# Denser gate scatter, and sparse rows of 2048 spread over peer_u and peer_v

## The reference

```python
idx = jnp.take_along_axis(cand_idx, pos, axis=-1)      # [256, 8, 16] experts
g = jax.nn.softmax(top_s, axis=-1)
u = expert_u[ic]
a = jnp.einsum('cd,ced->ce', xc, u)
w = gc * jax.nn.gelu(a)
y = jnp.einsum('ce,ced->cd', w, expert_v[ic])
```

## Time and profile before

| | us |
|---|---|
| median of 3 runs | 3195.71 (3194.75 to 3195.85) |
| profiled execution | 3201.04, its span 3199.2 |

### The profile page before, as it was taken

One profiled execution on the slowest core, in us unless ns is written; L12 is line 12 of the kernel. 1 busy time (PEld: TensorE's weight loads), 2 busy tenths in 40 slices (PEclk: granted clock), 3 DMA queues, 4 the chain that ended last, 5 costly groups with the idle time before them and its releaser, 6 DMA issues.

```text
span 3199.2 us, 44410 instructions
## 1 busy us (share of the span) xinstructions
PE 3096.1 (97%) x17208; PEld 2746.4 (86%) x17208; DVE 2202.6 (69%) x3156; ACT 1511.8 (47%) x2039; POOL 664.6 (21%) x499
## 2 busy tenths in 40 slices
PE   9889999999988779999999999999999999999998
PEld 7778899999888779999999988888888888888886
DVE  6776589997777368888876665655465655555556
ACT  5655455544344344444444544455444544444443
POOL 0010007776888732222210000000000000000000
PEclk9999999999999989999999999999999999999999
DMA  7465568889999689999877655555665666666664
GB/s 261 139 237 205 185 212 230 225 225 288 319 316 317 163 295 332 331 331 331 303 252 216 206 187 174 160 181 173 192 202 167 205 189 191 193 192 188 192 191 150
DMA packets 228019, 723.35 MB, mean 226 GB/s; under 512 B 55696, under 2 KB 64928, under 8 KB 218688
## 3 DMA queue, kind: packets, MB, share of 16 engines
q1 hardware_dynamic: 170784, 598.72, 57.7%
q0 software_dynamic: 56880, 121.75, 13.1%
q10 hardware_dynamic: 144, 0.05, 0.0%
HBM read 687.75 MB, written 31.57 MB: 225 GB/s over the span
## 4 chain that ended last, share of the span: by engine, by line
PE 76%; POOL 9%; DVE 8%; issue 4%; ACT 1%; DMA 1%; DVEq 0%; ACTq 0%; SPq 0%; POOLq 0%
PE PS L1928 75%; POOL scr_g L3150 8%; DVE wlo L2464 3%; PE PS L2023 1%; POOL M L3177 1%; ACT whi L2192 1%; DMA M<-scr_g 1%; DVE M L2787 0%; DMA scr_g<-M 0%; DVE TMP L2885 0%; DVE TMP L2879 0%; DVE M L2791 0%; DVE Y L2789 0%; DVE M L2785 0%; DVE M L2793 0%
## 5 line engine op out<-in xcount | busy, mean ns | idle before, releaser
L2464 DVE TENSOR_TENSOR wlo<-raw,whi 128x1024 fp32r<-128x1024 f32 x1101 | 1341.8, 1222 | 607.4 <-ACT whi L2192 604.9
L2192 ACT ACTIVATE whi<-raw 128x1024 fp32r<-128x1024 f32 x1101 | 1154.4, 1057 | 947.7 <-PE PS L1928 915.2
L1928 PE MATMUL PS<-BB,whi 128*128 128x448 f32 (+1 forms) x4352 | 1025.0, 378 | 30.8 <-ACT whi L2192 28.3
L1928 PEld LDWEIGHTS PS<-BB,whi 128*128 128x128 f32 x4352 | 787.2, 191 | 113.9 <-issue 31.3
L1928 PE MATMUL PS<-whi,AA 128*128 128x512 f32 x3072 | 780.5, 395 | 5.2 <-DVE AA L2518 1.8
L1928 PEld LDWEIGHTS PS<-whi,AA 128*128 128x128 f32 x3072 | 571.6, 188 | 122.9 <-DVE AA L2470 2.7
L1928 PEld LDWEIGHTS PS<-BB,wlo 128*128 128x128 f32 x4352 | 579.6, 192 | 56.9 <-DVE wlo L2464 32.9
L1928 PE MATMUL PS<-BB,wlo 128*128 128x224 f32 (+1 forms) x4352 | 585.4, 278 | 28.7 <-DVE wlo L2464 28.6
L3150 POOL DMA_INDIRECT scr_g<-M x256 | 452.7, 1768 | 92.2 <-issue 76.8
L1928 PE MATMUL PS<-wlo,AA 128*128 128x512 f32 x1536 | 417.4, 390 | 0.0
L1928 PEld LDWEIGHTS PS<-wlo,AA 128*128 128x128 f32 x1536 | 288.8, 188 | 61.0
(11 more groups left out here) (275 smaller groups left out, 1856.4 us busy)
## 6 DMA issues: line engine op xcount, KB each, us to landing
raw<-in_peer_u SPq DMA_DIRECT2D x256, 512.0 KB, 4.7
raw<-in_peer_v SPq DMA_DIRECT2D x256, 512.0 KB, 5.2
raw<-in_w_in SPq DMA_DIRECT2D x160, 512.0 KB, 3.7
raw<-in_w_up SPq DMA_DIRECT2D x128, 512.0 KB, 4.3
raw<-in_w_down SPq DMA_DIRECT2D x128, 512.0 KB, 4.3
raw<-in_w_out SPq DMA_DIRECT2D x64, 512.0 KB, 4.2
raw<-in_w_in_a SPq DMA_DIRECT2D x32, 512.0 KB, 4.4
raw<-in_peer_w_q SPq DMA_DIRECT2D x32, 512.0 KB, 4.4
```

What stands on the lines that cost most here:

```text
L1928: return e.matmul(outp, l, r, start=start, stop=stop)
L2192: e.activation(whi[:, n % NH, :], raw[:, n % NR, :], ACT.Copy).then_inc(s_hi, 1)
L2464: e.tensor_tensor(wlo[:, n % NH, :], raw[:, n % NR, :], bf(whi[:, n % NH, :]), ALU.subtract).then_inc(s_lo, 1)
```

## The change

- The gates and addresses of both go to one array `RG[t]`. For t = 1 a new step `pack_rows` on ACT's DMA queue, two steps after the routing of those heads, lays the 96 dense tokens' columns out over 128 partitions (`packs`), with 12 DMAs, and with 4 more does what `route_rows` did on POOL. A round of t = 1 is then 12 scatters of 128 rows instead of 16 of 96, so 224 in all. They wait for the packing to land.
- Dots and adds take 2048 columns in one instruction. `sparse_sum` disappears.
- `EARLY` = 22 of the 32 rows are dotted over peer_u, now at one step and then two steps for each row, the dot two rows behind its gather. The other 10 and gelu and gate move into `sparse_rest` over peer_v, ahead of the adds, with two buffers and 2 + 2 steps a row. The fetches wait for the first 22 dots instead of all 32.
- In peer_v the guard that waited for the adds stands before chunk 7, block 5, and `v_end` waits for them in its task.

```diff
+SETS = ((96, 32),)
+NSP = sum(n for _, n in SETS)
-    SCATTERS, DOT_PACE, ADD_PACE = 1.5, ((1, 1), (1, 1)), (2, 2)
+    SCATTERS, EARLY, PACE = 1.5, 22, ((1, 2), (2, 2))
...
-                    for k in range(16):
+                    n_k = 16 if t == 0 else TL // 8
+                    for k in range(n_k):
...
                         if t == 1:
-                            go("route_rows", g, fresh("POOL", routed[-1][2]))
-                            for _ in range(GSP):
+                            for _ in range(2):
+                                yield
+                            go("pack_rows", g, fresh("ACT", ready))
+                            for _ in range(sum(128 // n for _, n in groups) + sum(128 // n for _, n in SETS)):
                                 mark = landing(f"routes_landed{g}")
                             sp_routed[g] = mark
+                            ready = [mark]
+                        routed.append((t, 4 * g, ready))
...
+            def row_stream(table, cols, bufs, pace, start, use):
+                landed, lead = {}, len(bufs) - 1
+                free = {b: [start, last_row[0]] for b in bufs}
+                for n in range(len(cols) + lead):
+                    if n < len(cols):
+                        b = bufs[n % len(bufs)]
+                        go("gather", table, cols[n], b, fresh("POOL", sp_routed[0], sp_routed[1], t_z, free[b]))
+                        landed[n] = landing(f"rows_landed{b % 3}")
+                    for _ in range(pace[0]):
+                        yield
+                    if n >= lead:
+                        b = bufs[(n - lead) % len(bufs)]
+                        last_row[0] = use(cols[n - lead], b, landed[n - lead])
+                        free[b] = [last_row[0]]
+                    for _ in range(pace[1 + n % (len(pace) - 1)]):
+                        yield
...
+                yield from sparse_dots(0, EARLY, (0, 1, 2), PACE[0], bar)
+                early.append(last_row[0])
...
-                go("fetch", n, fresh("POOL", w, a_written[n], g_written, sp_weighed))
+                go("fetch", n, fresh("POOL", w, a_written[n], g_written, early))
...
+            def sparse_rest():
+                start = [bar, g_written, early]
+                yield from sparse_dots(EARLY, NSP, (2, 3), PACE[1], start)
+                go("sparse_gelu", fresh("ACT", last_row))
...
+                    yield from row_stream(1, cols, (2, 3), PACE[1], start, add)
...
-                if c == 7:
-                    while not sp_added:
+                for db in range(8):
+                    while (c, db) == (7, 5) and not sp_added:
                         step()
...
+            def pack_rows(g, ready):
+                for mark in ready:
+                    e.wait_ge(*mark)
+                rows = RG[1][:, 128 * g:128 * g + 128]
+                per = TL // 8
+                cols = packs[:, 8 * per * g:8 * per * g + 8 * per].rearrange("p (h c) -> p h c", h=8)
+                for q, n in groups:
+                    parts = rows.rearrange("p (h s r) -> p h s r", h=8, s=128 // n)
+                    for i in range(128 // n):
+                        e.dma_start(cols[n * i:n * i + n, :, q // 8:q // 8 + n // 8], parts[q:q + n, :, i, :]
+                                    ).then_inc(sem(f"routes_landed{g}"), 16)
...
+            def sparse_dot(m, b, ready):
+                for mark in ready:
+                    e.wait_ge(*mark)
+                x = row_bufs[b]
+                e.tensor_tensor_reduce(out=x, in0=x, in1=z_all, scale=1.0, scalar=0.0, op0=ALU.mult, op1=ALU.add,
+                                       accum_out=sp_dot[:, m:m + 1]).then_inc(sem("sparse_step"), 1)
```

More of the change, by code:

```diff
@@ L1239, in walk, with z_side @@
             bar, t_z, sp_weighed = [], [], []
-            def z_side():
+            last_row, z_of = [None], [None]
+            def z_side(i, b, start):
+                go("load_gain2", b, fresh("POOL", start, last_row))
+                a = landing("z_landed")
+                for _ in range(4):
+                    yield
+                go("z_rows", b, r2, fresh("DVE", t_r2, t_R, a, bar))
+                a = up("DVE", "sparse_step")
+                yield
+                go("z_spread", i, b, fresh("POOL", a, start, last_row))
+                for _ in range(128 // SETS[i][1]):
+                    mark = landing("z_landed")
+                t_z[:] = [a, mark]
+                z_of[0] = i
@@ new lines, in sparse_dots, with dot @@
+            def sparse_dots(first, end, bufs, pace, start):
+                def dot(m, b, landed):
+                    go("sparse_dot", m, b, fresh("DVE", landed, t_z))
+                    return up("DVE", "sparse_step")
+                for i in range(len(SETS)):
+                    cols = [m for m in range(first, end) if columns[m][0] == i]
+                    if cols and z_of[0] != i:
+                        yield from z_side(i, bufs[0], start)
+                    if cols:
+                        yield from row_stream(0, cols, bufs, pace, start, dot)
@@ L1242, in z_side, with first_dots @@
+            early = []
+            def first_dots():
                 while not bar:
                     yield
[L1244 to L1281, removed]
@@ L1397, in walk @@
                 if u == 59:
-                    while not sp_weighed or len(g_written) < 2:
+                    while not early or len(g_written) < 2:
                         step()
@@ L1408, in walk @@
             nA, sp_added = [], []
[L1410 to L1423, removed]
-                yield
[L1425 to L1429, removed]
-                    yield
[L1431 to L1434, removed]
@@ L1437, in walk, with v_end @@
+            tasks.append(sparse_rest())
             ssv = stat(16).rearrange("p (t c) -> p t c", t=2)
             r3, ss_v, t_r3, rows_in_place = stat(2), stat(2), [], []
-            def v_end(db, ready):
+            def v_end(db, summed):
                 k0 = 2 * db
+                while not sp_added:
+                    yield
+                ready = [summed, sp_added]
                 bank, bfree = yield from wait_for(misc)
@@ L2334, in gelu @@
                 act(gels[gi].rearrange("p (m n) -> p m n", m=2), usum[ti], ACT.Gelu_apprx_tanh, "gelu")
+            def pack_rows(g, ready):
[9 more added lines that the diff above has]
+                                    ).then_inc(sem(f"routes_landed{g}"), 16)
+                for j, (p0, n) in enumerate(SETS):
+                    both = rows[p0:p0 + n, :].rearrange("p (a s m) -> p a s m", a=2, s=128 // n)
+                    a = columns.index((j, 0)) + n // 2 * g
+                    for i in range(128 // n):
+                        e.dma_start(routes[n * i:n * i + n, :, a:a + n // 2], both[:, :, i, :]
+                                    ).then_inc(sem(f"routes_landed{g}"), 16)
             def sparse_gelu(ready):
@@ L3161, in z_spread @@
+            def z_spread(i, b, ready):
                 for mark in ready:
                     e.wait_ge(*mark)
-                for s in range(GSP):
-                    e.dma_start(z_all[NSP * s:NSP * s + NSP, :], u_rows[1][P0:128, :]).then_inc(sem("z_landed"), 16)
-            def route_rows(g, ready):
+                p0, n = SETS[i]
+                for k in range(128 // n):
+                    e.dma_start(z_all[n * k:n * k + n, :], row_bufs[b][p0:p0 + n, :]).then_inc(sem("z_landed"), 16)
@@ L3167, in route_rows, with gather @@
+            def gather(table, m, b, ready):
                 for mark in ready:
                     e.wait_ge(*mark)
[L3169 to L3179 removed]
```

142 lines of the change are left out of this document (71 added, 71 removed).

## The result

The changed kernel takes 3174.25 us (median of 5, 3165.67 to 3176.62), beside 3194.75 for the kernel before (median of 5). The ratio is 0.9925, with a 95% interval of 0.9914 to 0.9936: 20 to 28 us less. The forecast was 37 less.

The account below looks back on a forecast made before the run. POOL's queue of scatters and gathers was taken to bound peer_u. Its 74.7 us loss goes to 29 + 8, plus 1, minus 2: 37 less, 3159 us from 3195.71; likeliest 3145 to 3172, range 3133 to 3182.

Parts of the forecast that it names:

- Bound and mechanism: In peer_u, POOL's scatters and gathers set the pace (44.5 us lost) and end late at the tail (29.5 us lost).
- Scatters: On POOL, t = 1 goes from 128 scatters of 96 rows to 96 of 128: 224 in all, about 56 us less.
- Wait of a scatter: A POOL scatter waits for the rest of a running DVE dot or split: mean 0.43 us before, 0.50 after.
- A unit with dots: In peer_u, POOL needs 11.9 us a unit (bounds 10.5 and 12.1); 29 us lost replaces 44.5.
- Tail: At peer_u's end, last scatter about 1042 plus packing cost, before the gate is wanted; the 29.5 us gap goes.
- the better clock: In the first unit of peer_v, the chain of fetches keeps its steps; 1 us was given for TensorE's better clock.
- Packing: 16 DMA issues on ACT, twice, about 7 us each with 4.5 covered: 4 a time, 8 us, bounds 0 and 20.
- rival B: Packing costs much more (20 us) or POOL is still late at the fetch: 3182, middle 3176; chance 0.18.
- the sum: Over the whole kernel, 74.7 us goes to 29 + 8; plus 1, minus 2: 37 less, 3159.
- peer_v: 10 more gathers and dots, then 32 wide adds, done by u57; 0 to 8 us, taken as 2.
- rival C: Wide DVE instructions delay splits and stop TensorE, 78 us against 37 gained: slower, some 3235; chance 0.05.
- The observables: Expected signs: no gate wait, unit ends 11.9 apart, scatter mean near 2.0, some over 3 us, ACT blocks, peer_v 10.1 a unit.

Follow-up runs that it names:

- r5: The changed kernel with 1.6 scatters a step until the first gathers are planned and 1.25 after, for 1.5 throughout: 3156.71 us, ratio 0.9866.
- r2: The kernel before with only the dense packing and the 224 scatters, its dots untouched: 3198.73 us, ratio 0.9996.
- r3: The changed kernel with the old 256 scatters and rows laid out by POOL, nothing packed on ACT: 3195.12 us, ratio 0.9986.
- r8: The changed kernel with each dot of 2048 as two instructions of 1024, back to back: 3167.33 us, ratio 0.9895.
- r9: The changed kernel with every dot over the first 32 of 2048 columns only, gathers and waits kept: 3143.36 us, ratio 0.9827.
- r6: The changed kernel with the scatter rates of r5 and the packing issued four DMAs at a time: 3157.83 us, ratio 0.9847.
- r7: As r6, with the first expert gates planned after unit 60 of peer_u instead of 61: 3168.55 us, ratio 0.9906.
- r4: The changed kernel with the 16 packing DMAs issued four at a time in a task of their own: 3170.60 us, ratio 0.9911.
- r11: The changed kernel with 16 rows dotted over peer_u, dots in halves, 1.6 then 1.3 scatters a step, packing in one piece: 3148.56 us, ratio 0.9843.

## Why the prediction was right or wrong

**Bound and mechanism: right.** POOL's queue was the bound in peer_u, in its pace and in its tail. r5 shows it for the pace by changing nothing but the order of that queue; r2, r3 and the earlier trace rows show it for the tail.

**Scatters: 224, right.** 101 of them after the first gather in the plan; the trace has 94 between the gathers and 7 behind.

**Wait of a scatter: right mechanism, wrong law.** Predicted mean 2.04 (1.54 + 0.50), measured 1.87. The average over chance meetings came out for the kernel before. Worked out again from the dots and splits in each trace, as an estimate, it gives 2.02 for the changed kernel (1.87 measured), 2.07 for r5 (2.09), 1.93 for r8 (1.86) and 1.84 for r9 (1.68): right once, and otherwise 0.07 to 0.16 high. So the meetings aren't left to chance. What sets them isn't shown; the gathers of r6 are the clearest sign that the two queues can fall into step. What dots cost POOL in all is in r9: 0.18 a scatter and 0.46 a gather.

**A unit with dots: right by luck.** 11.9 predicted for POOL's work from one gather to the next, 11.83 measured, and 30.0 lost for 29. Errors cancel in it. Scatters were cheaper than predicted (0.8 us a unit), gathers dearer (1.55 for 1.3), and 6.6 us of waits between rounds of one kind were not in the sum.

**Tail: right.** Last scatter predicted at 1042 plus the packing's cost, measured at 1052.09. (The first fetch of the kernel before stands at 1121.37 in the prediction; that is the first of `scr_g`, and one of `scr_a` went out at 1120.76, from which the table counts.) The 29.5 us went. The first unit of peer_v kept its stall and took 28.3 us, 27.6 before, so the 1 us that I gave it for the better clock didn't come. (The 24 us that r7's expectation has for this unit were a misreading.)

**Packing: the mis-sized term.** 8 predicted, 16 measured (7.8 and 8.3). Two things are in it. An issue takes 0.66 and not the 0.40 of the earlier trace rows, so ACT was blocked 9.57 and not 7; 4.2 of that were covered, close to the 4.5 that I had counted on, and TensorE stood 5.33. And the clock after that standing, which I had put at nothing, cost 2.7 more (4.78 and 1.5 in the second of the two units). The 1 us a time that I added because DVE can't make up what it loses was a guess at the wrong thing. This is the mechanism of rival B, which had 20. Counted stage by stage the packing makes up 8 of the 10.6 us missing between 37.7 and 27.1 in peer_u; the rest is 1 in the units with dots and 2 elsewhere. But by r4 a smaller packing cost wouldn't have made the kernel faster, so this entry isn't why the gain fell short.

**The step that failed in kind: the sum.** I added what packing, dots and tail cost as if each stood alone. r4 shows that with no packing cost the kernel is no faster (the units with dots then lose 40 for 26), and r2 and r3 that each half alone is worth 1 to 4 us and both together some 24. While one queue paces two stretches, time saved on TensorE before or in the first is waited for in the next.

**peer_v: right in size.** 2 predicted; 2.2 measured between u63 and the next stage, with 0.7 of it in the first unit. After that unit TensorE's waits for DVE sum to 2.7 us in the changed kernel, and the kernel before has none in the matmuls. Most of them are for the gated values (`AA`, `BB`) and none for `wlo`, so rival C's mechanism isn't there.

**The observables.** No wait at the gate, 10.1 a unit over peer_v, blocks on ACT and scatters over 3 us are all there. The mean near 2.0 isn't. Nor are unit ends 11.9 apart: from u36 to u58 they are 11.46 apart on average, 10.1 up to u45 and 12.4 after it. The prediction's own loss of 29 us in 22 units already meant 11.4.

## What to carry to other kernels

When an engine's queue is the bound over two stretches, sum the queue from its first instruction to the one that others wait for, and compare that with the time the other engines need; terms taken stretch by stretch don't add up, and halves of such a change tested alone can each look worthless. Put work on that queue at a rate that leaves it ahead at the point where somebody begins to wait for it. And before moving DMA issues to a queue that also computes, count them all at the price that one of them has on that queue, and add to the time that TensorE stands what its clock costs afterwards. Spreading them takes the stop away, but gains time only where no other queue is the bound.

## What the runs showed of the hardware that was not expected

- A DMA issue on ACT in the packing took 0.66 us (six in 3.94), against 0.40 for the one of 128 pieces of 368 bytes. Small pieces don't explain it: the four issues with pieces of 64 bytes took 0.64 each (2.57), those with 16 bytes 0.66. What does isn't shown. Sixteen in a row held ACT for 9.6 us.
- After TensorE had stood for 5.33 us it was granted 0.50 for some 5 us, and that cost 2.7 us on top. Of the 30 us lost with dots some 12 are work at a lower granted clock too, by the estimate above.
- A scatter on POOL waits for the rest of the DVE dot or split (both have two inputs in SBUF) that is running when it starts: 1.68 us over its free time beside a dot of 2.29, at most about 1.1 beside ones of 1.22 (longest scatter 2.59 in r8). Between two such instructions back to back it gets in. A gather waits too: 1.01 us when it starts beside none, 2.09 on average beside one in the changed kernel.
- The mean of a scatter doesn't follow their number: 2.09 us in r5 with 3.75 planned a unit, 1.87 in the changed kernel with 4.5, and 1.87 in r11 with 3.9 and dots in halves. How the two queues lie against each other counts as much.
- The same kernel's times can spread by 30 us of 3150 (r6, four executions), while the kernel before keeps within 16. That POOL being near the pace is the reason is likely, but not shown: r5, near it too, keeps within 9.
